# Inverse levels of the scan packed to 32 columns, with zero-padded 64x64 stationary blocks and the last level across row groups

## The chip, the cores and the metric

The kernel runs on one core of one Trainium2 chip. The metric is the device time of one execution in microseconds, the median of several runs. Engines are named as in the profile: PE (matrix products, PEld its weight loads), DVE (vector), ACT (scalar), POOL (GpSimd) and SP, which issues most DMAs. Each engine works through its own instructions in order; between engines there are only semaphores.

## What is computed

Two layers of a decoder trunk over 512 tokens of width 1024. Layer 0 mixes tokens with RWKV-7 (8 heads of 64) and gated DeltaNet (8 heads of 64), layer 1 with two kinds of attention, and each layer ends in a squared-ReLU MLP. The change touches only the chunked form of the two recurrences of layer 0. For a chunk of 64 tokens the reference of the DeltaNet half says:

```
a_mat = where(strict, einsum('bhnik,bhnjk->bhnij', k_beta, k) * decay, 0) + eye(C)
tri = partial(triangular_solve, left_side=True, lower=True, unit_diagonal=True)
u = tri(a_mat, v * beta);  w = tri(a_mat, k_beta * exp(g))
```

The kernel forms the inverse of the unit triangular 64x64 matrix instead of solving, for both recurrences: R stands for the RWKV half and G for the DeltaNet half. There are 8 heads x 2 chunks in a tile of 128 partitions x 512 columns (a chunk on each half of the partitions, a head on each 64 columns).

## The kernel before

Layer 0 first projects the inputs: 31 tiles of weights are loaded by SP, rounded by ACT (`tile_hi`, L1045), the rest of the split is computed by POOL (`tile_lo`, L1984), and PE multiplies. Between `tile_lo(3)` and `tile_lo(6)` POOL also builds constants: triangular masks in FULL, 128 partitions square for each of LEVELS = 6 levels, and from them MERGE, whose 64x64 blocks are copied for each half of the partitions (L2018 to L2021). SP loads tile u only after `tile_lo(u - 2)`.

Then comes the scan, `for s in range(TT + 1)` with TT = 4. Each engine has this loop with the calls written out by hand. In step s the products and the inverse of token block s are made ("ahead") while the state of block s - 1 is carried on and its output is made ("behind"). Step 0 has nothing behind, step 4 nothing ahead. The order on each engine is the order of the calls.

The inverse of a block doubles the size of the inverted diagonal blocks per level. The start is Q = I - (L within blocks of two): DVE multiplies L by the mask MERGE[0] (L1630 for G, L1641 for R) and POOL adds the identity (L2052), DVE transposes it into T (L1652). `LAST` is 5. For `lev` 0 to 4:

- PE, `below_blocks`: X = L x T, in PSUM bank 0 for R and bank 1 for G (through `both_halves`, L640: 8 heads x 2 halves of 64x64 times 64x64)
- ACT, `below_blocks` (L1189): copy of X with factor -1, one instruction of 128x512 for each of R and G
- PE, `joined_blocks`: Q x X, into the same bank
- DVE, `joined_blocks`: `copy_predicated` under MERGE[lev + 1] into T (L1659), for R then G; then, but for the last level, the transposes of R and G into Q (L1664). The last level writes straight into Q, which raises inv_done.

`both_halves` also makes key_values, MKV (L1175 on ACT evicts it), and chunk_out. `head_products` (L632) makes the four raw products, `by_state` (L655), `one_half` (L648) and `outer` (L744) serve the state. On ACT, L1171 evicts the lower rows of R, L1184 the state reads, L1199 and L1201 compute the norms of the output with a table load each, L1207 and L1211 scale and evict the turned output. On DVE, L1635, L1639 and L1640 mask the products, L1682 to L1685 update the state, L1698 to L1704 begin the chunk output, L1611 and L1612 scale the next rows. SP loads the first weights of the output projection only after inv_done of the last block.

Of the kernel before, what the change touches and what calls it, by code (L numbers as in the profile page):

```python
# [29 lines left out]
P = 128  # L30
# [67 lines left out]
def trunk_kernel(nc, a, out):  # L98
    ctx = ExitStack()
    with ctx:  # L100
# [54 lines left out]
        MERGE = grid(o_merge, LEVELS, HD)  # L155
        INCLC, STRICTC, EYEC = (flat(o_merge + (LEVELS + i) * HD, HD) for i in range(3))
# [88 lines left out]
        LTR, LTG, TIR, TIG, XMR, XMG, DT = (by_head(home("inverse")) for _ in range(7))  # L245
# [8 lines left out]
        MK = DT  # L254
        QC_KC, AD_RD = flat(o_gqkv, 8 * W), flat(o_kk, 8 * W)
# [59 lines left out]
        def p_reads(q):  # L315
# [44 lines left out]
        (inv_m, inv_q0, inv_x, inv_xm, inv_y, inv_t, inv_q, inv_done) = (sem(n) for n in (  # L360
            "inv_m inv_q0 inv_x inv_xm inv_y inv_t inv_q inv_done").split())
# [121 lines left out]
        def _(pe):  # L483
# [213 lines left out]

            def below_blocks(s, lev):

                n = 2 * LAST * s + 2 * lev  # L700
                for g, (lt, ti) in enumerate(((LTR, TIR), (LTG, TIG))):
                    pe.wait_ge(inv_t, n + (2 if lev == 0 else g + 1))
                    both_halves(g, lt, ti, True).then_inc(inv_x, 1)

            def joined_blocks(s, lev):
                n = 2 * LAST * s + 2 * lev
                for g, (qi, xm) in enumerate(((QIR, XMR), (QIG, XMG))):
                    pe.wait_ge(inv_xm, n + g + 1)
                    if lev == 0:
                        pe.wait_ge(inv_q0, 2 * s + 2)  # L710
                    else:
                        pe.wait_ge(inv_q, 2 * (LAST - 1) * s + 2 * (lev - 1) + g + 1)
                    if lev < LAST - 1:
                        both_halves(g, qi[s % 2], xm, True).then_inc(inv_y, 1)
                    else:
                        both_halves(g, xm, qi[s % 2], True).then_inc(inv_y, 1)
# [279 lines left out]
        def _(act):  # L996
# [221 lines left out]
            for s in range(TT + 1):  # L1218
# [195 lines left out]
        def _(dve):  # L1414
# [206 lines left out]
            def gated_products(s):  # L1621
# [8 lines left out]
                dve.tensor_tensor(QIG[s % 2], LTG, mask(MERGE[:, 0, :]), mul).then_inc(inv_m, 1)  # L1630
# [6 lines left out]
            def key_products(s):  # L1637
# [3 lines left out]
                dve.tensor_tensor(QIR[s % 2], LTR, mask(MERGE[:, 0, :]), mul).then_inc(inv_m, 1)  # L1641
# [481 lines left out]
```

## Time and profile before

| | |
|---|---|
| median of 3 runs | 1543.94 us (1543.9 to 1547.18) |
| profiled execution | 1542.63 us, its span 1540.7 us |
| mean granted clock of PE | 0.97 of full |
| busy: PE, PEld | 1440.3 us (93%), 1153.7 us |
| busy: DVE, ACT, POOL | 677.3, 605.4, 571.3 us |
| `L640 PE MATMUL 64*64 64x64 f32`, inputs in lower | x2112, 73.4 us busy, mean 228 ns |

A row of the timeline is the start, the time, the engine, the line, the operation with its shapes, and in square brackets how long the engine stood idle before it and who released it. "x2" merges instructions that follow one another; their time is then that of the run. An operation of fp32 on PE shows as two records, so that a group of `both_halves` has 32. The scan lies between about 220 and 442 us of the span. Steps 0 to 3 begin about 220, 255, 305 and 356 us.

### The profile page before, as it was taken

The page shows a single profiled execution, that of the slowest core. Times are in us where ns is not written, and L with a number is a line of the kernel's source. Part 1 is how long each engine was busy: PE and PEld are TensorE (multiplying, and loading weights), DVE is VectorE, ACT ScalarE, POOL GpSimd, SP SyncE. Part 2 cuts the span into 40 slices and gives each one's busy share as a digit, 9 for nine tenths or more (in the row PEclk, how much of TensorE's full clock was granted, in tenths as well). Part 3 has the DMA queues.
Part 4 walks back from the last instruction along what each step waited for, and adds up shares of the span by engine and source line. Part 5 has one row for each costly group of instructions (what it writes and reads, how often), then busy time and mean ns, then how long its engine had stood idle before and what let it go on. Part 6 is the DMA issues. An engine that isn't in the chain of part 4 may idle for free.

```text
span 1540.7 us, 24474 instructions
## 1 busy us (share of the span) xinstructions
PE 1440.3 (93%) x10273; PEld 1153.7 (75%) x10273; DVE 677.3 (44%) x1059; ACT 605.4 (39%) x872; POOL 571.3 (37%) x265
## 2 busy tenths in 40 slices
PE   7999899888769999999999799978999999999998
PEld 5787568788758888888888687754468888888886
DVE  4675756777543413223143306868823314122231
ACT  5425453434354413223142435467834313232231
POOL 4543321101024343434334232417934343434341
PEclk9999899999779999999999899998999999999999
DMA  4332200000112323232323221210012323223231
GB/s 141 96 96 68 69 14 3 3 3 3 57 55 84 108 84 107 83 100 91 107 84 83 82 83 56 82 55 1 1 55 83 109 82 104 88 93 97 85 106 54
DMA packets 128392, 109.99 MB, mean 71 GB/s; under 512 B 10679, under 2 KB 126513, under 8 KB 128305
## 3 DMA queue, kind: packets, MB, share of 16 engines
q1 hardware_dynamic: 127712, 107.64, 22.6%
q8 instruction: 69, 1.13, 0.3%
q10 hardware_dynamic: 592, 1.07, 0.2%
q14 instruction: 19, 0.15, 0.0%
HBM read 106.60 MB, written 2.10 MB: 71 GB/s over the span
## 4 chain that ended last, share of the span: by engine, by line
PE 76%; DVE 11%; ACT 5%; POOL 3%; issue 3%; DMA 1%; DVEq 0%; ACTq 0%; SPq 0%; POOLq 0%
PE ps L503 21%; PE ps L508 21%; PE ps L504 21%; PE ps L640 5%; POOL lower L2093 2%; DVE lower L1880 2%; DVE lower L1876 1%; PE ps L655 1%; PE ps L648 1%; POOL pw_lo L1984 1%; DVE lower L1865 1%; ACT lower L1377 1%; PE ps L744 1%; PE ps L617 1%; PE ps L540 1%
## 5 line engine op out<-in xcount | busy, mean ns | idle before, releaser
L2061 POOL TENSOR_TENSOR w_lo<-lower,w_hi 128x2048 fp32r<-128x2048 f32 x84 | 387.8, 4616 | 634.7 <-ACT w_hi L1033 634.7
L503 PE MATMUL ps<-h_hi,w_hi 128*128 128x512 f32 x792 | 316.3, 399 | 8.9 <-ACT h_hi L1038 5.9
L504 PE MATMUL ps<-h_hi,w_lo 128*128 128x512 f32 x792 | 315.0, 398 | 0.0
L1033 ACT ACTIVATE w_hi<-lower 128x2048 fp32r<-128x2048 f32 x84 | 160.2, 1907 | 242.8 <-PE ps L508 242.8
L508 PE MATMUL ps<-h_lo,w_hi 128*128 128x512 f32 x792 | 201.6, 396 | 0.3
L503 PE MATMUL ps<-a_hi,w_hi 128*128 128x512 f32 x480 | 189.3, 394 | 0.0
L504 PE MATMUL ps<-a_hi,w_lo 128*128 128x512 f32 x480 | 189.2, 394 | 0.0
L503 PEld LDWEIGHTS ps<-h_hi,w_hi 128*128 128x128 f32 x792 | 150.5, 190 | 46.4 <-issue 11.5
L504 PEld LDWEIGHTS ps<-h_hi,w_lo 128*128 128x128 f32 x792 | 150.6, 190 | 36.0 <-issue 0.5
L508 PEld LDWEIGHTS ps<-h_lo,w_hi 128*128 128x128 f32 x792 | 148.9, 188 | 37.2 <-DVE h_lo L1582 1.7
L1825 DVE TENSOR_TENSOR lower<-lower,ps 128x512 f32<-128x512 f32 x64 | 44.0, 688 | 268.7 <-PE ps L508 268.7
L1809 DVE SCALAR_TENSOR_TENSOR lower<-ps,lower 128x512 f32<-128x512 f32 x64 | 44.3, 692 | 226.0 <-PE ps L508 209.9
L1264 ACT ACTIVATE lower<-lower 128x512 f32<-128x512 f32 x64 | 40.5, 633 | 215.9 <-DVE lower L1809 215.9
L508 PE MATMUL ps<-a_lo,w_hi 128*128 128x512 f32 x480 | 121.5, 395 | 0.0
L1984 POOL TENSOR_TENSOR pw_lo<-lower,pw_hi 128x1024 fp32r<-128x1024 f32 (+1 forms) x31 | 76.2, 2460 | 118.4 <-ACT pw_hi L1045 118.2
L508 PEld LDWEIGHTS ps<-a_lo,w_hi 128*128 128x128 f32 x480 | 90.3, 188 | 21.6
L504 PEld LDWEIGHTS ps<-a_hi,w_lo 128*128 128x128 f32 x480 | 90.2, 188 | 21.2
L503 PEld LDWEIGHTS ps<-a_hi,w_hi 128*128 128x128 f32 x480 | 90.1, 188 | 21.1
L1814 DVE TENSOR_TENSOR h_lo<-lower,h_hi 128x512 fp32r<-128x512 f32 x64 | 97.4, 1521 | 6.9 <-ACT h_hi L1266 6.9
L503 PE MATMUL ps<-x_hi,pw_hi 128*128 128x512 f32 (+1 forms) x232 | 94.4, 407 | 0.4 <-POOL pw_lo L1984 0.4
L504 PE MATMUL ps<-x_hi,pw_lo 128*128 128x512 f32 (+1 forms) x232 | 91.5, 394 | 0.0
L640 PE MATMUL ps<-lower 64*64 64x64 f32 x2112 | 73.4, 228 | 11.6 <-DVE lower L1659 7.9
(356 smaller groups left out, 1974.0 us busy)
## 6 DMA issues: line engine op xcount, KB each, us to landing
lower<-in_mlp_w_dram SPq DMA_DIRECT2D x64, 1024.0 KB, 5.4
lower<-in_ev_w_in_dram SPq DMA_DIRECT2D x30, 512.0 KB, 3.9
lower<-in_od_w_in_dram SPq DMA_DIRECT2D x10, 1024.0 KB, 5.1
lower<-in_ev_w_out_dram SPq DMA_DIRECT2D x4, 1024.0 KB, 5.1
lower<-in_od_w_out_dram SPq DMA_DIRECT2D x4, 1024.0 KB, 4.9
out_dram<-lower SPq DMA_DIRECT2D x4, 512.0 KB, 3.2
lower<-in_od_w_in_dram SPq DMA_DIRECT2D x6, 256.0 KB, 3.8
upper<-in_x_dram SPq DMA_DIRECT2D x1, 1024.0 KB, 7.2
```

Of the source, the lines that this page charges most:

```text
L503: pe.matmul(o, wh, xh, start=(i_ == 0), stop=False)
L504: pe.matmul(o, wl, xh, start=False, stop=False)
L508: mm = pe.matmul(o, wh, xl, start=False, stop=(i_ == n_ - 1))
L640: mm = pe.matmul(ps[part, b, h_ * HD:(h_ + 1) * HD], mats[part, j, q, :], vals[part, j, q, :], start=(start and h_ == 0), stop=True, skip_ ...
L1033: act.activation(WH[:, u % 2, :, 0:w], RAW[:, u % 2, :, 0:w], ACT.Copy).then_inc(hi_ready, 1)
L1264: act.activation(sq, sq, ACT.Square).then_inc(h1_sq, 1)
L1809: dve.scalar_tensor_tensor(out=SQT[:, b % 4, :], in0=src(q)[:, :], scalar=0.0, in1=RS[2 * l + 1], op0=ALU.max, op1=mul).then_inc(bank_read, 1)
L1814: dve.tensor_tensor(HL[:, b, :], SQT[:, b % 4, :], as_f32(HH[:, b, :]), sub).then_inc(h1_ready, 1)
L1825: dve.tensor_tensor(XT[:, k, :], XT[:, k, :], src(q_m2[l] + k)[:, :], add)\
L1880: t.step(dve.match_replace(sc, M8[:, i, :], sc, TAKEN))
L1984: pool.tensor_tensor(PWL[:, u % 3, :, 0:w], PRAW[:, u % 2, :, 0:w], as_f32(PWH[:, u % 3, :, 0:w]), ALU.subtract).then_inc(pw_lo, 1)
L2061: pool.tensor_tensor(WL[:, u % 2, :, 0:w], RAW[:, u % 2, :, 0:w], as_f32(WH[:, u % 2, :, 0:w]), ALU.subtract)\
```

## The change

The diagonal 32x32 blocks are kept in compact form: Q (QCR, QCG) and its transpose (TCR, TCG) have 32 columns for each head, 128x256 in all, in place of 128x512. L is spread once into LDR and LDG, 64x64 per head, with zeros off the two diagonal 32x32 blocks; that is done on ACT by `sides`, two instructions with a factor of 0 or 1 for each partition (SIDE). In the inner levels (0 to 3) PE multiplies 64x64 stationary blocks with 32 moving columns (`in_halves`); ACT evicts X by `sides` with factors 0 and -1, again as a padded block, which becomes the stationary side of the second product. `copy_predicated` goes into the compact Q, and the transpose of that gives the moving side of the next level. In the last level PE works with 32x32 blocks that lie in different row groups (`across`), ACT copies compactly and then expands both Q into full width (four instructions, inv_exp), and DVE copies the lower left block in.

New ahead of the levels: ACT `diagonal` (a copy for each of G and R; the one for G stands before L1171 and waits for r_kk) and `spread` (four instructions, behind the eviction of MKV and before `solved(m, 1)`); DVE `diagonal` (a predicated copy and a multiplication for G behind L1635, for R behind L1640), where L1630 and L1641 go; POOL's addition becomes half as wide and also waits for inv_ld. POOL's constants lose the sixth level and the copies of MERGE, and gain JOIN, EYEQ and SIDE.

```diff
-        MERGE = grid(o_merge, LEVELS, HD)
-        INCLC, STRICTC, EYEC = (flat(o_merge + (LEVELS + i) * HD, HD) for i in range(3))
+        INCLC, STRICTC, EYEC = (flat(o_merge + i * HD, HD) for i in range(3))
+        HQ = HD // 2
+        JOIN = grid(o_merge + 3 * HD, LEVELS - 1, HQ)
+        EYEQ = flat(o_merge + 3 * HD + (LEVELS - 1) * HQ, HQ)
+        SIDE = flat(o_merge + 3 * HD + LEVELS * HQ, 4)
...
+            def in_halves(b, mats, vals):
+                for h_ in range(NH):
+                    j, q = h_ // 2, h_ % 2
+                    for part in HALVES:
+                        mm = pe.matmul(ps[part, b, h_ * HQ:(h_ + 1) * HQ], mats[part, j, q, :], vals[part, j, q, :],
+                                       start=True, stop=True)
+                return mm
+
+            def across(b, mats, vals, down):
+
+                for h_ in range(NH):
+                    j, q = h_ // 2, h_ % 2
+                    for k in range(2):
+                        first, second = (slice(k * HD + i * HQ, k * HD + (i + 1) * HQ) for i in range(2))
+                        rows, cols = (first, second) if down else (second, first)
+                        mm = pe.matmul(ps[cols, b, h_ * HQ:(h_ + 1) * HQ], mats[rows, j, q, :], vals[rows, j, q, :],
+                                       start=True, stop=True)
+                return mm
+
             def below_blocks(s, lev):
 
                 n = 2 * LAST * s + 2 * lev
-                for g, (lt, ti) in enumerate(((LTR, TIR), (LTG, TIG))):
+                for g, (lt, ld, tc) in enumerate(((LTR, LDR, TCR), (LTG, LDG, TCG))):
                     pe.wait_ge(inv_t, n + (2 if lev == 0 else g + 1))
-                    both_halves(g, lt, ti, True).then_inc(inv_x, 1)
+                    if lev < LAST - 1:
+                        pe.wait_ge(inv_ld, 2 * s + 2)
+                        in_halves(g, ld, tc).then_inc(inv_x, 1)
+                    else:
+                        across(g, lt[:, :, :, HQ:HD], tc, True).then_inc(inv_x, 1)
...
+            def sides(dst, src, neg, done):
+                act.activation(dst[:, :, :, 0:HQ], src, ACT.Copy, scale=SIDE[:, neg:neg + 1])
+                act.activation(dst[:, :, :, HQ:HD], src, ACT.Copy, scale=SIDE[:, neg + 1:neg + 2]).then_inc(done, 1)
+
+            def diagonal(s, g, lt, qc):
+                act.wait_ge(r_kk if g else r_lt, s + 1)
+                act.activation(qc, lt[:, :, :, 0:HQ], ACT.Copy).then_inc(inv_a, 1)
+
+            def spread(s):
+                for g, (ld, qc) in enumerate(((LDG, QCG), (LDR, QCR))):
+                    act.wait_ge(inv_c, 2 * s + g + 1)
+                    sides(ld, qc, 0, inv_ld)
+
             def below_blocks(s, lev):
-                for g, xm in enumerate((XMR, XMG)):
+                for g, (xe, ld) in enumerate(((QIR[s % 2], LDR), (QIG[s % 2], LDG))):
                     act.wait_ge(inv_x, 2 * LAST * s + 2 * lev + g + 1)
-                    act.activation(flat4(xm), bank[g], ACT.Copy, scale=-1.0).then_inc(inv_xm, 1)
+                    if lev < LAST - 1:
+                        sides(xe, quarter(g), 2, inv_xm)
+                    else:
+                        act.activation(compact(ld), quarter(g), ACT.Copy, scale=-1.0).then_inc(inv_xm, 1)
+                if lev == LAST - 1:
+                    for g, (qi, qc) in enumerate(((QIR[s % 2], QCR), (QIG[s % 2], QCG))):
+                        act.wait_ge(inv_q, 2 * (LAST - 1) * s + 2 * (LAST - 2) + g + 1)
+                        sides(qi, qc, 0, inv_exp)
...
                 if ahead:
+                    diagonal(s, 1, LTG, QCG)
                     lower_rows(s)
+                    diagonal(s, 0, LTR, QCR)
                     key_values(s)
+                    spread(s)
...
+            def diagonal(s, g, lt, qc, tc):
+                dve.wait_ge(inv_a, 2 * s + g + 1)
+                dve.copy_predicated(qc, on_side(1), lt[:, :, :, HQ:HD]).then_inc(inv_c, 1)
+                dve.wait_ge(inv_c, 2 * s + g + 1)
+                dve.tensor_tensor(tc, qc, of_quarter(JOIN[:, 0, :]), mul).then_inc(inv_m, 1)
...
             def joined_blocks(s, lev):
                 n = 2 * LAST * s + 2 * lev
                 inner = lev < LAST - 1
-                for g, x in enumerate((TIR, TIG) if inner else (QIR[s % 2], QIG[s % 2])):
+                for g, (qc, qi) in enumerate(((QCR, QIR[s % 2]), (QCG, QIG[s % 2]))):
                     dve.wait_ge(inv_y, n + g + 1)
-                    dve.copy_predicated(x, blocks(MERGE[:, lev + 1, :]), by_head(bank[g]))\
-                       .then_inc(inv_t if inner else inv_done, 1)
+                    if inner:
+                        dve.copy_predicated(qc, of_quarter(JOIN[:, lev + 1, :].bitcast(I32)), quarter(g))\
+                           .then_inc(inv_q, 1)
+                    else:
+                        dve.wait_ge(inv_exp, 2 * s + g + 1)
+                        dve.copy_predicated(qi[:, :, :, HQ:HD], on_side(0), quarter(g)).then_inc(inv_done, 1)
                 if inner:
-                    for g, (ti, qi) in enumerate(((TIR, QIR), (TIG, QIG))):
-                        dve.wait_ge(inv_t, n + 2 + g + 1)
-                        dve.transpose(flat4(qi[s % 2]), flat4(ti)).then_inc(inv_q, 1)
+                    for g, (tc, qc) in enumerate(((TCR, QCR), (TCG, QCG))):
+                        dve.wait_ge(inv_q, 2 * (LAST - 1) * s + 2 * lev + g + 1)
+                        dve.transpose(flat4(tc), flat4(qc)).then_inc(inv_t, 1)
...
             for part in HALVES:
-                t.link(pool.tensor_copy(MERGE[part], FULL[part, :, part]))
                 t.link(pool.tensor_copy(INCLC[part], INCL[part, part]))
                 t.link(pool.tensor_copy(EYEC[part], IDENT[part, part]))
             t.link(pool.tensor_tensor(STRICTC, INCLC, EYEC, ALU.subtract))
+            for i in range(4):
+                rows = slice(i * HQ, (i + 1) * HQ)
+                t.link(pool.tensor_copy(JOIN[rows], FULL[rows, 0:LEVELS - 1, rows]))
+                t.link(pool.tensor_copy(EYEQ[rows], IDENT[rows, rows]))
+                for at_, v_ in enumerate((1 - i % 2, i % 2, i % 2 - 1, -(i % 2))):
+                    t.link(pool.memset(SIDE[rows, at_:at_ + 1], float(v_)))
```

## Rows read from the trace of the kernel before

**Rows 1.** Chain that ended last, 200 to 470 us: start, time, what
```profile
230.95 1.28 POOL upper L2052
...
233.03 21.32 PE ps L640 x640
```

**Rows 2.** Timeline of ACT, 262 to 306 us (step 1): start, time, engine, line, operation
```profile
263.61 1.02 ACT L1184 ACTIVATE lower<-ps 64x1024 f32<-64x1024 f32 x1 [0.36 <-PE ps L655]
...
283.95 0.60 ACT L1189 ACTIVATE lower<-ps 128x512 f32<-128x512 f32 x1 [6.48 <-PE ps L640]
...
287.80 0.60 ACT L1189 ACTIVATE lower<-ps 128x512 f32<-128x512 f32 x1 [2.32 <-PE ps L640]
...
300.27 1.07 ACT L1189 ACTIVATE lower<-ps 128x512 f32<-128x512 f32 x2
301.22 1.51 ACT L1207 ACTIVATE lower<-ps,lower 128x128 f32<-128x128 f32 x4
302.59 0.72 ACT L1211 ACTIVATE upper<-ps,lower 128x512 f32<-128x512 f32 x1
```

**Rows 3.** Timeline of DVE, 285 to 308 us (step 1)
```profile
285.81 0.73 DVE L1659 COPY_PREDICATED lower<-lower,ps 128x512 f32<-128x512 int32 x1 [3.97 <-PE ps L640]
286.75 0.73 DVE L1659 COPY_PREDICATED lower<-lower,ps 128x512 f32<-128x512 int32 x1 [0.20 <-PE ps L640]
287.37 1.29 DVE L1664 STREAM_TRANSPOSE lower<-lower 128x512 f32<-128x512 f32 x2
288.59 0.65 DVE L1698 TENSOR_TENSOR lower<-lower 128x512 f32<-128x512 f32 x1
...
292.61 1.33 DVE L1659 COPY_PREDICATED lower<-lower,ps 128x512 f32<-128x512 int32 x2
```

**Rows 4.** Timeline of POOL, 38 to 50 us (constants)
```profile
39.22 0.55 POOL L1967 TENSOR_SCALAR_AFFINE_SELECT lower<-lower 128x64 f32<-128x64 f32 x2
...
42.19 0.60 POOL L2013 MEMSET lower<- 128x1 f32 x16
...
43.02 0.50 POOL L2018 COPY lower<-lower 64x384 f32<-64x384 f32 x1
...
43.88 0.23 POOL L2020 COPY lower<-lower 64x64 f32<-64x64 f32 x1
...
45.79 4.78 POOL L1984 TENSOR_TENSOR pw_lo<-lower,pw_hi 128x1024 fp32r<-128x1024 f32 x2
```

**Rows 5.** Chain that ended last, 38 to 62 us
```profile
50.60 5.11 DMA lower<-in_ev_w_in_dram
...
58.93 3.24 PE ps L579 x7
```

**Rows 6.** Timeline of PE, 106.6 to 107.45 us
```profile
106.82 0.39 PE L586 MATMUL ps<-lower 128*128 128x32 f32 x2
107.13 0.43 PE L589 MATMUL ps<-lower 128*64 128x32 f32 x8
```

**Rows 7.** Records of L589: duration min/median/max ns, first and last start us, form
```profile
L589 PE MATMUL ps<-lower x8: 222/223/243, 107.1 to 107.3; 128*64 128x32 f32 x8
```

**Rows 8.** Timeline of DVE, 262 to 275 us (step 1, ahead of the levels)
```profile
266.33 0.43 DVE L1683 TENSOR_TENSOR upper<-upper,lower 128x256 f32<-128x256 f32 x1
266.68 0.41 DVE L1685 TENSOR_TENSOR upper<-upper,ps 128x256 f32<-128x256 f32 x1
...
267.86 0.68 DVE L1640 TENSOR_TENSOR upper<-ps,lower 128x512 f32<-128x512 f32 x1
```

**Rows 9.** Timeline of PE, 226 to 240 us (step 0)
```profile
230.42 1.94 PE L640 MATMUL ps<-upper,lower 64*64 64x64 f32 x32 [1.50 <-DVE upper L1640]
...
233.03 3.68 PE L640 MATMUL ps<-lower 64*64 64x64 f32 x64 [0.66 <-DVE lower L1652]
...
238.81 1.39 PE L640 MATMUL ps<-lower 64*64 64x64 f32 x40
```

**Rows 10.** Stretches: time, busy of PE, PEld, DVE, ACT, POOL, granted clock, DMA, GB/s
```profile
230.00:235.00 5.00, 3.92 (x69) 3.76 (x70) 2.21 (x4) 0.60 (x1) 2.27 (x2) 0.55 0.01 3
...
340.00:345.00 5.00, 2.17 (x48) 2.03 (x46) 4.93 (x10) 1.26 (x2) 0.00 (x0) 0.81 0.02 3
```

More of the change, by code:

```diff
@@ L242, in of_tokens @@
             return x[:, :, s * P:(s + 1) * P].rearrange("p j (q t) -> p j q t", q=2)
-        LTR, LTG, TIR, TIG, XMR, XMG, DT = (by_head(home("inverse")) for _ in range(7))
+        LTR, LTG, LDR, LDG, DT = (by_head(home("inverse")) for _ in range(5))
+        QCR, QCG, TCR, TCG = (home("inverse", 2 * P).rearrange("p (j q t) -> p j q t", j=PAIRS, q=2) for _ in range(4))
         GTRI = by_head(home("even"))
@@ L254, in trunk_kernel, with compact, quarter @@
         MK = DT
+        def compact(x):
+            return x.rearrange("p j q t -> p (j q t)")[:, 0:2 * P].rearrange("p (j q t) -> p j q t", j=PAIRS, q=2)
+        def quarter(b):
+            return bank[b][:, 0:2 * P].rearrange("p (j q t) -> p j q t", j=PAIRS, q=2)
         QC_KC, AD_RD = flat(o_gqkv, 8 * W), flat(o_kk, 8 * W)
@@ L359, in trunk_kernel @@
              "e_sqg e_sqr e_var e_ln e_rstd e_on r_tr r_tg").split())
[L360 to L361 removed]
+        (inv_a, inv_c, inv_ld, inv_m, inv_q0, inv_x, inv_xm, inv_y, inv_t, inv_q, inv_exp, inv_done) = (
+            sem(n) for n in "inv_a inv_c inv_ld inv_m inv_q0 inv_x inv_xm inv_y inv_t inv_q inv_exp inv_done".split())
         LAST = LEVELS - 1
@@ L1998, in _ @@
             select(first, 0, [[-2, P // 2]], 1, 0.0, ALU.is_equal)
-            for lev in range(1, LEVELS):
+            for lev in range(1, LEVELS - 1):
                 if lev == 3:
@@ L2002, in _ @@
                 b = 1 << lev
-                last = int(lev == LEVELS - 1)
-                low = FULL[:, lev, :].rearrange("p (n q w) -> p n q w", q=2, w=b)[:, :, last, :]
-                t.link(pool.memset(low, 1.0))
-                select(low, 0 if last else -b, [[-2 * b, P // (2 * b)], [0, b]], 1, 0.0)
-                select(low, b - 1 if last else 2 * b - 1, [[2 * b, P // (2 * b)], [0, b]], -1, 0.0)
+                right = FULL[:, lev, :].rearrange("p (n q w) -> p n q w", q=2, w=b)[:, :, 1, :]
+                t.link(pool.memset(right, 1.0))
+                select(right, 0, [[-2 * b, P // (2 * b)], [0, b]], 1, 0.0)
+                select(right, b - 1, [[2 * b, P // (2 * b)], [0, b]], -1, 0.0)
             tile_lo(5)
@@ L2049, in _ @@
                     pool.memset(SG, 0.0).then_inc(e_state, 1)
-                for g, qi in enumerate((QIG, QIR)):
+                for g, (qc, tc) in enumerate(((QCG, TCG), (QCR, TCR))):
                     pool.wait_ge(inv_m, 2 * s + g + 1)
-                    pool.tensor_tensor(qi[s % 2], qi[s % 2], of_heads(EYEC), ALU.add).then_inc(inv_q0, 1)
+                    pool.wait_ge(inv_ld, 2 * s + g + 1)
+                    pool.tensor_tensor(qc, tc, EYEQ.unsqueeze(1).unsqueeze(1).broadcast_to([P, PAIRS, 2, HQ]),
+                                       ALU.add).then_inc(inv_q0, 1)
                 if s < TT - 1:
```

26 lines of the change are left out of this document (12 added, 14 removed).

## The prediction

> **What bounds the kernel now.** I read the chain of work that ended last, then each engine in order of time. The scan of layer 0 (about 220 to 442 us) is the only stage whose arithmetic changes. In the chain it is mostly L640, the helper behind all products of the inverse [rows 1]: in step 0 one piece of 21.32 us holds the whole inverse. So in step 0 every microsecond counts, while in steps 1 to 3 other work lies between the levels. One level repeats every 3.85 us (283.95 to 287.80 on ACT) [rows 2]; the four groups of products in it take 0.93 us each (two copies on DVE, each released by its group, start at 285.81 and 286.75) [rows 3], so 3.73 of 3.85 us are PE. A small gain of DVE or ACT is worth nothing there unless PE gets faster, and any stretch of latency is paid at once. A second place matters: POOL. The constants that it builds between two weight splits fill it from 42.19 to 45.79 us [rows 4], and the chain goes on from them through the next splits, a load of 5.11 us and ACT to PE's L579 [rows 5].
>
> **Constants, on the path.** POOL now builds four JOIN copies (32 partitions x 160), four EYEQ copies (x 32) and sixteen one-column memsets, each waiting for the one before. The 64x384 copy took 0.50 us and the 64x64 copy 0.23 [rows 4], so 0.31 and 0.20, with 0.06 us between links; a one-column memset is 0.10 (16 of them overlapped in 0.60, with 0.04 between starts) [rows 4], linked 0.16. Added: 4 x (0.37 + 0.26) + 16 x 0.16 = 5.1 us. Gone: two big copies (2 x 0.56) and the sixth mask, whose two selects took 0.55 [rows 4] and its memset with the links 0.3. Net 3.1 us in front of the split at 45.79. Behind it the chain goes from the second split straight to the load and on [rows 5], and PE's later tiles only queue behind L579. So I take all of it: **+3.1**. Bounds: 1.5, if one-column links cost half, to 4.
>
> **The products.** Each fp32 product shows as two records, 32 records a group. Inner levels keep a 64x64 stationary block and halve the moving columns to 32. The trace has that shape: L589, 64 columns stationary and 32 moving, 8 records in 0.43 us [rows 6]; one record is 0.22 [rows 7], so the three steps between its four pairs are 0.07 each, the first, which starts the stream, the longest. L586 has 128 stationary and 32 moving columns: two records in 0.39, some 0.11 to 0.16 apart by the same reckoning [rows 6]. The pitch follows the stationary width, not the moving one, and today's group with 64 moving columns is 16 pairs in 0.93, 0.058 each. So I take 0.93 for an inner group after the change, too: **no gain on PE**. The other bound is 0.47, if in this tiling the moving side sets it. In the last level the blocks are 32 wide: 0.47 by width, 0.93 by count. I take 0.6.
> For that last level a rule speaks against a gain: the Trainium skill, "TensorEngine Tiling (Array Packing)", Instruction Overhead, says that a matmul of one column takes as long as one of 60 and that a dimension already small should not be tiled. As an estimate from that page, 60 cycles for each of 32 records is 0.8 us at full clock instead of my 0.6; the sum would be 0.8 us higher (two groups on the path in steps 0 and 3). No row here has this shape.
>
> **The inner cycle.** Dependencies change: `copy_predicated` now fills the compact QC, and the moving operand TC is its transpose. DVE's order is copy R, copy G, transpose R, transpose G, so the next level waits for both copies and a transpose; before, it waited for copy R alone. DVE: a 128x256 operation is 0.41 to 0.43 with 0.35 between starts, 0.27 less than the 0.68 of a 128x512 [rows 8]; the 512-wide copy and transpose are 0.73 and 0.68 [rows 3], so 0.46 and 0.42. ACT: one eviction of 0.60 becomes two with a per-partition scale. Such a 128x512 is 0.72; 512 columns more cost 0.43 (1.02 against 0.59 to 0.60), so 256 less give 0.50; four 128x128 take 1.51, 0.35 apart [rows 2], so with 128 columns more 0.40 between starts and 0.9 us for both. From the start of a level: group R lands at 1.15, ACT to 2.08, joined R 2.13 to 3.28; joined G starts at 3.07 and lands at 4.17; copy G at 4.22, transpose R 4.58 to 5.00, next level at 5.04. That is **+1.19 per level** where nothing covers it.
>
> **Step 0, uncovered.** (a) ACT's new copy waits for r_kk, and behind it in its queue stands L1171, the lower rows, for which L1635 waits: +0.45. DVE then does copy and multiply for G (0.85, 0.1 of it slack) before L1639: key values on PE start at 231.6 instead of 230.42 [rows 9]. They land at 233.5 (cold clock), ACT copies MKV (0.6, 0.48 to the next start), then spreads L (4 x 0.40 + 0.1): 235.8; POOL adds the identity in 0.75 (1.27 for double width [rows 1]); transpose: the first level starts at 237.1 instead of 233.03 [rows 9]: **+4.05**. (b) Level 0 ran mostly at a clock near half (0.55 [rows 10]; 64 records in 3.68 us [rows 9]) and took 5.78 us. The new cycle is 8.1 cold (groups of 1.75) and 5.04 warm; if the clock rises about 4 us after PE restarts, as it did, 6.9: **+1.1**. (c) Levels 1 to 3: 3 x 1.19 = **+3.6**. (d) Last level: smaller evictions, copies and products: **-0.5** (0 to -0.9). Sum 8.2.
>
> **Steps 1 to 3.** (a) Front: the new copy on ACT pushes L1171 back by 0.3; on DVE copy and multiply (0.85) stand before the state sums, so L1640 ends at 269.35, not 268.54 [rows 8]; PE's key values wait for that: +0.81. The mask multiply L1630 that falls away was hidden behind ACT. Queued behind are the chunk's state reads, which move with it. The spread on ACT (to 273.0) and POOL's add lie in PE's work until 275.6 and cost nothing; if that cover went, 1 us. (b) Level 0: ACT +0.29. (c) Level 1 is 1.19 longer on PE, but level 2 is bound by DVE's chunk output: from L1698 (288.59) to the copy at 292.61, 4.02 us [rows 3]. L1698 can start 5.26 us after level 1 instead of 5.77, since copies and transposes are narrower; then 4.02 and 1.19 to the next level: 10.48 instead of 10.57, so -0.09, and both extra waits of PE are hidden. (d) After level 3 ACT's two table loads and exponentials bound the step (up to 300.27 [rows 2]), and that eviction is 0.28 later: +0.28. (e) At the end DVE's two copies go from 1.33 [rows 3] to 0.82, unless the last products or the four new expansions on ACT (4 x 0.40) come later, which today are not there: -0.1 to -0.5, taken -0.35. That is **+0.94** each for steps 1 and 2. In step 3 PE was last at the end, so the cheaper last level gives -0.7: **+0.6**.
>
> **Sum**: 3.1 + 8.2 + 1.9 + 0.6 = 13.8 us. The profiled execution took 1542.63 us (span 1540.7): 1556.4. The three runs have median 1543.94, 1.3 above it; I forecast **1556.5**.
>
> **Rivals.**
> 1. *The moving side sets the pace*: inner groups 0.47. For: 64 and 32 are both half of something here and L589 is only 8 records. Against: L586 and L589 [rows 6, 7]. The cycle is then 4.10 (step 0: 3 x 0.25; ACT and DVE bound it), step 0 costs 4.5, steps 1 to 3 give back 1.1 each because L1698 starts 1.4 earlier: 3.1 + 4.5 - 3.3 = +4.3, **1547**.
> 2. *The clock falls*: PE now stands about 1 us in every level. The granted clock fell in step 2 after a stand of 2.8 us (0.81 in 340 to 345 [rows 10]), but not in step 1 after the same stand. At the low level a cycle is 8.1, 3.0 more. One more cold level a step is +12: **1568**; all of them near +30. It decides where the gaps together make PE count as idle. The reverse is in it, too: the stand before level 3 shrinks from 2.8 to about 1.4 us, and the two falls of steps 2 and 3, 1.4 us each, could go: 1553.6, inside my forecast.
> 3. *Faster*: rival 1, with POOL's constants covered by a load that lands sooner, and the two clock falls of steps 2 and 3 gone: 4.3 - 3.1 - 2.9 = -1.7 against the profile's 1542.6, and with step 0's spread overlapped by PE's cold products 2 less, **1539**. Against it: the chain through POOL [rows 5]. It wins once groups are at 0.5 or less.
> 4. *The change doesn't do what it says*: the narrower DVE work is all on covered stretches and so are the additions; within 2 us, **1545**.
>
> **How the numbers follow.** Forecast with its clock variant 60% (1551 to 1561 for itself), rival 1 12%, rival 2 15%, rival 3 7%, rival 4 6%. The range leaves out the deep end of rival 2, rival 3 and half of rival 4: 1545.5 to 1568. Against 1543.94, 0.2% (3.1 us, what a measurement can tell) puts faster at 7%; within at 11% (rival 4 and the low half of rival 1), slower at 82%.
>
> **What would show it.** Groups of L640's successor: evictions of R and G 0.93 apart in inner levels (step 1, level 1) if the stationary side binds, under 0.6 if not. In step 0 a level every 5.0 us. PE's first level of step 0 some 4 us later after its key values than now, after the fourth spread on ACT. The split behind POOL's constants near 48.9 instead of 45.79, and L579 as much later. Level 3 of step 1 no later relative to level 1. What would make it wrong: groups at half length, a clock near 0.5 through the levels, or POOL's one-column links far from 0.16 us.

## The result and the profile after

The changed kernel takes **1599.28 us** (median of 4 runs, 1595.2 to 1602.73) against 1543.92 for the kernel before, measured beside it: 1.0355 times as long, with a 95% interval of 1.0329 to 1.0382. I had forecast 1556.5, at most 1568. The direction was right, the size was not: 43 us are missing from the sum. The profiled execution took 1602.73 us with a span of 1601.0 and a mean granted clock of 0.924 (0.97 before); it is the slowest of the four, so sums over its steps come to 60 us of loss where the medians give 55.

In what follows a stand is a stretch of time in which PE has nothing to do and waits for another engine, and a fall is a stretch in which its granted clock goes from 1.00 to 0.50.

The first thing to look at is the clock. Stretches of step 0, the kernel before and then the kernel after (columns as in [rows 10]):

```profile
240.00:250.00 10.00, 10.00 (x342) 9.92 (x338) 7.17 (x12) 4.31 (x8) 0.16 (x1) 1.00 0.02 5
```
```profile
240.00:250.00 10.00, 9.12 (x172) 8.99 (x172) 1.54 (x4) 2.48 (x6) 0.00 (x0) 0.50 0.01 2
250.00:260.00 10.00, 9.12 (x173) 8.99 (x170) 2.13 (x5) 2.55 (x7) 0.00 (x0) 0.50 0.01 3
260.00:270.00 10.00, 9.12 (x170) 8.96 (x168) 1.99 (x5) 2.84 (x6) 1.82 (x2) 0.50 0.01 2
```

PE is busy for 9.12 of 10 us, but it issues half as many records, at a granted clock of 0.50, which is its level of 1.2 GHz. Before, the clock was back at 1.00 from 237.3 us on and stayed there until 343.1, in step 2. The timeline of PE in the kernel after shows the levels that follow from it; they answer to [rows 9]:

```profile
239.31 3.62 PE L713 MATMUL ps<-lower 64*64 64x32 f32 x64 [3.62 <-DVE lower L1712]
...
247.23 3.63 PE L713 MATMUL ps<-lower 64*64 64x32 f32 x64 [0.88 <-DVE lower L1728]
...
255.15 3.63 PE L713 MATMUL ps<-lower 64*64 64x32 f32 x64 [0.88 <-DVE lower L1728]
...
270.99 3.46 PE L724 MATMUL ps<-lower 32*32 32x32 f32 x128 [0.88 <-DVE lower L1728]
275.61 2.05 PE L677 MATMUL ps<-upper,lower 128*128 128x512 f32 x2 [1.16 <-DVE upper L1724]
```

A level repeats every 7.92 us. It is the cold cycle of my sum (8.1) in all four inner levels, where I had the clock rise within the first. From the second level on each has a stand of 0.88 us in front of it, which DVE's transpose ends.

Two other views answer to [rows 2] and [rows 4]. ACT in step 1, a level at full clock, and POOL at the constants:

```profile
313.59 0.47 ACT L1217 ACTIVATE lower<-ps,lower 128x256 f32<-128x256 f32 x1 [10.22 <-PE ps L713]
313.96 0.47 ACT L1218 ACTIVATE lower<-ps,lower 128x256 f32<-128x256 f32 x1
314.53 0.47 ACT L1217 ACTIVATE lower<-ps,lower 128x256 f32<-128x256 f32 x1
```
```profile
44.89 0.31 POOL L2088 COPY lower<-lower 32x160 f32<-32x160 f32 x1
45.26 0.20 POOL L2089 COPY lower<-lower 32x32 f32<-32x32 f32 x1
45.52 0.53 POOL L2091 MEMSET lower<- 32x1 f32 x4
...
49.82 0.12 POOL L2092 MEMSET lower<- 128x16 f32 x1
50.01 4.71 POOL L2050 TENSOR_TENSOR pw_lo<-lower,pw_hi 128x1024 fp32r<-128x1024 f32 x2
```

The groups of R and G are 0.94 us apart (313.59 to 314.53): 32 moving columns gain nothing at full clock.

The table gives, for each profiled run, the start of the scan (PE's first product of step 0, L666 or its like), the length of each step from one such product to the next, steps 3 and 4 together up to DVE's first operation on the finished rows, the rest of the span, and how long the clock was at 0.50 between 215 and 530 us by the clock record. The kernels are those of the experiments below. The medians are over all executions, the other columns are of the one that was profiled.

| kernel | median us | scan starts | step 0 | 1 | 2 | 3 and 4 | rest | at 0.50 |
|---|---|---|---|---|---|---|---|---|
| before | 1543.9 | 220.0 | 35.2 | 49.9 | 51.4 | 86.7 | 1097.5 | 44 |
| after | 1599.3 | 223.0 | 52.6 | 63.4 | 65.2 | 99.2 | 1097.7 | 195 |
| e1 | 1569.1 | 222.9 | 42.0 | 55.0 | 54.8 | 94.6 | 1097.5 | 92 |
| e2 | 1570.3 | 220.5 | 47.2 | 54.5 | 54.5 | 94.2 | 1097.7 | 116 |
| e3 | 1562.8 | 223.8 | 40.3 | 54.4 | 54.6 | 91.1 | 1097.6 | 85 |
| e4 | 1548.7 | 225.8 | 34.8 | 49.9 | 51.3 | 86.7 | 1097.4 | 41 |
| e5 | 1568.1 | 223.1 | 43.7 | 54.2 | 54.6 | 93.3 | 1096.0 | 75 |
| e6 | 1558.1 | 224.1 | 40.6 | 55.0 | 54.5 | 85.6 | 1095.8 | 31 |
| e7 | 1537.6 | 221.8 | 33.3 | 51.4 | 51.4 | 82.8 | 1095.3 | 10 |
| e8 | 1541.4 | 223.2 | 37.8 | 51.4 | 51.1 | 80.8 | 1095.2 | 7 |
| e9 | 1532.3 | 221.4 | 33.3 | 49.9 | 49.9 | 81.4 | 1095.9 | 0 |
| e10 | 1551.6 | 220.9 | 35.4 | 50.2 | 54.6 | 90.1 | 1097.4 | 58 |
| e11 | 1546.3 | 223.6 | 37.8 | 53.3 | 52.3 | 83.8 | 1094.5 | 27 |
| e12 | 1546.6 | 224.0 | 40.5 | 51.4 | 50.6 | 81.7 | 1096.7 | 3 |
| e13 | 1567.3 | 223.1 | 49.9 | 55.8 | 57.4 | 84.6 | 1094.6 | 72 |
| e14 | 1591.7 | 223.7 | 49.7 | 58.3 | 58.3 | 99.2 | 1096.8 | 150 |

Nearly all of the loss lies in the scan: 3.0 us ahead of it, 17.4, 13.5, 13.8 and 12.5 in the steps, 0.2 behind. And the time at 0.50 grew by 150 us. The start of the scan alone lies between 220.0 and 221.8 us in the five kernels whose work ahead of it is that of before, so the 3.0 is good to about 1 us.

### The profile page after: what moved, and what is told of

Read it like the earlier page. It is cut to its first block, busy times and chain, and to the rows that moved or that the text cites. A ratio compares the mean times of both kernels' runs of the same rounds, so it can differ in the third digit from the quotient of the medians.

```text
span 1601.0 us, 24581 instructions
## 1 busy us (share of the span) xinstructions
PE 1491.4 (93%) x10273; PEld 1201.3 (75%) x10273; DVE 659.5 (41%) x1067; ACT 627.0 (39%) x944; POOL 570.0 (36%) x284
## 4 chain that ended last, share of the span: by engine, by line
PE 77%; DVE 10%; ACT 6%; POOL 3%; issue 2%; DMA 1%; DVEq 0%; ACTq 0%; SPq 0%; POOLq 0%
PE ps L519 20%; PE ps L514 20%; PE ps L515 20%; PE ps L713 6%; POOL lower L2165 2%; DVE lower L1946 1%; PE ps L666 1%; DVE lower L1942 1%; PE ps L651 1%; PE ps L628 1%; PE ps L659 1%; ACT lower L1430 1%; PE ps L724 1%; POOL pw_lo L2050 1%; DVE lower L1931 1%
## 5 line engine op out<-in xcount | busy, mean ns | idle before, releaser
L1317 ACT ACTIVATE lower<-lower 128x512 f32<-128x512 f32 x64 | 40.5, 633 | 215.9 <-DVE lower L1875 215.9
L515 PEld LDWEIGHTS ps<-a_hi,w_lo 128*128 128x128 f32 x480 | 90.1, 188 | 21.4
L515 PE MATMUL ps<-x_hi,pw_lo 128*128 128x512 f32 (+1 forms) x232 | 91.1, 393 | 0.0
L713 PE MATMUL ps<-lower 64*64 64x32 f32 x1536 | 74.9, 268 | 11.6 <-DVE lower L1728 7.9
```

Of the source, the lines that this page charges most:

```text
L515: pe.matmul(o, wl, xh, start=False, stop=False)
L713: mm = pe.matmul(ps[part, b, h_ * HQ:(h_ + 1) * HQ], mats[part, j, q, :], vals[part, j, q, :], start=True, stop=True)
L1317: act.activation(sq, sq, ACT.Square).then_inc(h1_sq, 1)
```

## The experiments

**e1: the columns sent twice.** In the changed kernel:

```diff
-                        mm = pe.matmul(ps[part, b, h_ * HQ:(h_ + 1) * HQ], mats[part, j, q, :], vals[part, j, q, :],
+                        mm = pe.matmul(ps[part, b, h_ * HD:(h_ + 1) * HD].rearrange("p (a t) -> p a t", a=2),
+                                       mats[part, j, q, :],
+                                       vals[part, j, q, :].unsqueeze(1).broadcast_to([HD, 2, HQ]),
```

> The changed kernel, with each inner product of the inverse sent its 32 moving columns twice (64 columns into the full bank, of which ACT and DVE read the first 32 of each 64). The work that is used, the waits and the order are those of the changed kernel. Theory 1, the granted clock stays at 0.50 because only 32 columns move behind each 64-wide stationary block: the clock is back at 1.00 from the second level of step 0 on, as before the change, an inner level of step 0 takes 5.0 to 5.1 us, and the time is my forecast's sum, 1553 to 1560 us. Theory 2, the stands of 0.9 us that the longer chain of DVE and ACT leaves in every level make the clock fall: the stands are still there, so the clock stays at 0.50 and the time within 5 us of 1599. Theory 3, the padded blocks themselves cost the time: also near 1599.

Measured: 1569.11 us, 1.0152 (1.0124 to 1.0181). More work for PE, and 30 us less time. Stretches of step 0, and its levels on PE:

```profile
240.00:250.00 10.00, 9.11 (x248) 8.69 (x244) 2.00 (x5) 3.35 (x8) 0.00 (x0) 0.85 0.01 3
250.00:260.00 10.00, 8.23 (x258) 7.76 (x256) 3.68 (x9) 4.37 (x10) 0.45 (x1) 1.00 0.01 3
```
```profile
245.89 2.08 PE L716 MATMUL ps<-lower 64*64 64x64 f32 x64 [0.88 <-DVE lower L1733]
...
250.94 2.08 PE L716 MATMUL ps<-lower 64*64 64x64 f32 x64 [0.88 <-DVE lower L1733]
...
261.03 2.38 PE L729 MATMUL ps<-lower 32*32 32x32 f32 x128 [0.88 <-DVE lower L1733]
```

The clock is back at 1.00 and a level takes 5.05 us, with the same stands of 0.88. Theory 1 holds for step 0 but not in its time, and theories 2 and 3 fall. 13 us above my sum remain: the clock still falls, most of all near the step ends (263 to 270, 315 to 325, 369 to 380) and for 48 us from 424 us on.

**e2: only the columns halved, in the kernel before.** Half of each inner product is left out. `in_halves` is here the loop of `both_halves` with `vals[part, j, q, 0:HD // 2]` as its moving side, and the inner levels of `joined_blocks` go through it, too:

```diff
-                    both_halves(g, lt, ti, True).then_inc(inv_x, 1)
+                    (in_halves(g, lt, ti) if lev < LAST - 1 else both_halves(g, lt, ti, True)).then_inc(inv_x, 1)
```

> The kernel before, with the inner products (levels 0 to 2 and 3 of 5, all but the last) sent only the first 32 of their 64 moving columns; half of each inner product is left out, and the output is not the reference's. No wait, no order and no operation of another engine changes, and PE still stands for nothing between the groups of a level. Theory 1: a group at full clock keeps its 0.93 us (no gain from fewer columns), but in step 0 the clock doesn't rise to 1.00 after its first level as it does before the change, and much of the four inverses runs at 0.50: slower than before, 1565 to 1590 us. Theory 2 (stands decide): the clock is that of before, and the time 1544 within 3 us. Theory 4, the moving side sets the pace of a group: groups near 0.5 us and the time below 1541.

Measured: 1570.26 us, 1.0165 (1.0143 to 1.0186). Half of the columns taken away, no wait added, 26 us lost. Stretches and timeline of PE in e2:

```profile
240.00:250.00 10.00, 10.00 (x194) 10.00 (x191) 5.13 (x8) 1.79 (x3) 0.00 (x0) 0.50 0.01 2
250.00:260.00 10.00, 10.00 (x192) 10.00 (x192) 3.25 (x5) 2.95 (x5) 1.12 (x1) 0.50 0.02 3
```
```profile
257.44 3.60 PE L702 MATMUL ps<-lower,upper 64*64 64x32 f32 x64
260.86 3.66 PE L640 MATMUL ps<-lower 64*64 64x64 f32 x64
264.31 2.53 PE L640 MATMUL ps<-upper,lower 64*64 64x64 f32 x64
```

From 235 to 260 us PE is busy without a pause and the clock stays at 0.50. It rises at 265.4 us, inside the last level, which still has 64 columns. So once PE is at the low clock, these products with 32 columns did not bring it back here.

**e3: DVE's order, on top of e1.** In `joined_blocks` on DVE:

```diff
                            .then_inc(inv_q, 1)
+                        dve.wait_ge(inv_q, 2 * (LAST - 1) * s + 2 * lev + g + 1)
+                        dve.transpose(flat4((TCR, TCG)[g]), flat4(qc)).then_inc(inv_t, 1)
...
-                if inner:
-                    for g, (tc, qc) in enumerate(((TCR, QCR), (TCG, QCG))):
-                        dve.wait_ge(inv_q, 2 * (LAST - 1) * s + 2 * lev + g + 1)
-                        dve.transpose(flat4(tc), flat4(qc)).then_inc(inv_t, 1)
```

> The same as the kernel with its columns sent twice, and DVE's order in the inner levels is copy R, transpose R, copy G, transpose G, so that the next level waits for one copy and one transpose. The stand of PE between two levels goes from about 0.9 to 0.2 us. Theory 1: an inner level of step 0 takes about 4.4 us instead of 5.05, three of them count, and the time is 1 to 3 us under that kernel's, with the clock alike. Theory 2: the clock is low where the stands are 0.9 and full here, so this one is some 40 us faster than the other.

Measured: 1562.75 us, 1.0103 (1.0075 to 1.0131), 6.4 us under e1. An inner level takes 4.26 us. The gain is more than the 1 to 3 us of theory 1 and far from the 40 of theory 2: 1.7 in step 0 and 3.5 in steps 3 and 4, where less time is at 0.50.

**e4: POOL's constants alone, in the kernel before.** Behind its `tensor_tensor(STRICTC, ...)`:

```diff
+            for i in range(4):
+                rows = slice(i * HQ, (i + 1) * HQ)
+                t.link(pool.tensor_copy(JOIN[rows], FULL[rows, 0:LEVELS - 1, rows]))
+                t.link(pool.tensor_copy(EYEQ[rows], IDENT[rows, rows]))
+                for at_, v_ in enumerate((1 - i % 2, i % 2, i % 2 - 1, -(i % 2))):
+                    t.link(pool.memset(EYEQ[rows, at_:at_ + 1], float(v_)))
```

> The kernel before, and on POOL, in the place where the change builds them, the added constants alone: four copies of 32 x 160, four of 32 x 32 and sixteen linked one-column memsets, 5.1 us by my prices, with nothing removed. My forecast's step: all of it lies on the path, since the chain goes through POOL's next split, so the time is +4.5 to +5.5 us, 1548.5 to 1549.5. The rival: the loads of weights cover it, and the time is that of before within 1 us.

Measured: 1548.66 us, 1.0031 (1.0021 to 1.0041), +4.5 us; the added operations took 4.95 us on POOL and the steps of the scan are those of before. The step of my forecast holds: nothing covers them.

**e5: the last level twice, on top of e3.** In `across`:

```diff
-                        mm = pe.matmul(ps[cols, b, h_ * HQ:(h_ + 1) * HQ], mats[rows, j, q, :], vals[rows, j, q, :],
+                        for again in range(2):
+                            mm = pe.matmul(ps[cols, b, h_ * HQ:(h_ + 1) * HQ], mats[rows, j, q, :],
```

> The kernel with its columns sent twice and DVE in the order copy R, transpose R, copy G, transpose G (1562.75 us), and in addition each small product of the last level is issued twice, into the same place. A group of the last level goes from about 0.53 to 1.06 us at full clock, near the 0.93 that it took before the change; nothing else changes. In the kernel without this the clock fell to 0.50 for 10 us around the last level of steps 0 to 2 (279 to 290, 314 to 324, 368 to 378 in its trace) and for 20 and 17 us at the end. Theory 1, the small last level takes away work that kept the clock up: these falls go, except those that the kernel before had, too; steps 1 and 2 take 51 to 52 us instead of 54.5, and the time is 1552 to 1557, although PE does 2 us more in each step. Theory 2, the falls come from the stands at the end of a step and not from the small products: the clock falls as it did and the time is 1562 to 1567.

Measured: 1568.06 us, 1.0165 (1.0147 to 1.0183). Theory 1 fails: the falls at 279, 314 and 368 us went, others came (265 to 271, 336 to 347, 374 to 381), and 5 us were lost. Theory 2 comes within 1.1 us with its time (1562 to 1567), but its reason doesn't hold, as the falls did not stay where they were.

**e6: filler on top of e5.** The same function serves all later kernels:

```diff
+            def filler(b, n):
+                for i in range(n):
+                    pe.matmul(bank[b][:, 0:P], HEADS2, IDENT, start=True, stop=True)
```

It is called ahead of a wait, as `filler(7, 6)` in front of `pe.wait_ge(r_lt, s + 1)`, with a bank whose readers are done.

> The kernel of the run with the last level twice, and in addition products that nobody reads (128 columns, HEADS2 by IDENT, into a bank that is free) in the stands of PE: 5, 2, 10 and 16 ahead of the first level of step 0, 6 ahead of level 3 in steps 1 to 3, a few at the step ends, 10, 5 and 3 in the last chunk, 44 and 12 behind it. By 0.21 us each they fit into the stands. It shows what the change costs once the clock is held. Theory 1: the mean granted clock of the scan is near 1.00, what is left over the kernel before is the longer front of step 0, the longer cycle and POOL's constants, and step 0 takes 38 to 40 us: 1543 to 1550. Theory 2, the clock isn't moved by such work or the filler delays what it stands before: 1555 or more.

Measured: 1558.07 us, 1.0097 (1.0081 to 1.0114). That is theory 2's time, but not its first reason: the filler does move the clock, 31 us at 0.50 instead of the 75 of e5, and 10 us are won. Steps 3 and 4 are short (85.6), but steps 1 and 2 still take 55.0 and 54.5: PE's stands ahead of the key values are open, with 7, 10 and 10 us at 0.50 from about 15 us into each of steps 1 to 3, and the last level is doubled.

**e7: filler in the kernel before.**

> The kernel before with the same kind of filler in PE's stands: 5, 2, 6 and 6 ahead of the first level of step 0, 12 (2.6 us in a stand of 2.8) ahead of level 3 in steps 1 to 3, 3 and 2 at the step ends, 10, 5 and 3 in the last chunk, 44 behind it and 12 before the output projection. The kernel before spends 44 us of the scan at 0.50: 230 to 237, 343 to 347, 394 to 398, 411 to 425 and 432 to 449. Theory 1, work of any use keeps the clock: these go, at 3.4, 1.7, 1.7, about 5 and 3 us, and the time is 1528 to 1536. Theory 2, the clock is cut by power or time and not by what PE does: the falls stay or move elsewhere, and the time is 1542 to 1548.

Measured: 1537.56 us, 0.9961 (0.9947 to 0.9975). The clock follows the filler: 10 us at 0.50 instead of 44. The time misses my range by 1.6, since a new fall of 3.4 us came in each of steps 1 to 3, behind the stands that I had left open.

**e8: the change with every stand filled** (e3 and filler; 9 products ahead of the key values of steps 1 to 3 and 3 ahead of the second chunk's solved values).

> The change with its columns sent twice, DVE in the order copy R, transpose R, copy G, transpose G, the last level's products issued once, and the filler of the run before, to which 9 products ahead of the key values of steps 1 to 3 (a stand of 2.3 us there) and 3 ahead of each second chunk's solved values (0.9 us) are added. In every version of the change so far level 0 of steps 1 to 3 started 22.9 to 25.9 us after its step, against 19.56 before the change, with a fall of the clock in each. Theory 1, my forecast's front (+0.81) is right by itself and the fall of the clock is what it triggers, since PE's stand ahead of the key values grows by it: with the stand filled the clock holds, level 0 starts at 20.4 to 20.8, steps 1 and 2 take 50.5 to 51.5 us, and the time is 1545 to 1551. Theory 2, the front is longer by another wait: level 0 starts after 22.5 even at full clock, and the time is 1553 or more.

Measured: 1541.44 us, 0.9984 (0.9975 to 0.9993), 21 us under e3 and less than expected. Theory 1 holds: 7 us at 0.50 in the whole scan, and the first level of steps 1 to 3 starts 20.35, 21.45 and 20.34 us after the step's first product (19.56 before the change; the fall of 7 us lies in step 1's end and step 2's start).

**e9: the kernel before with every stand filled.**

> The kernel before with the filler of the earlier run (1537.56 us, clock low for only 3.4 us in each of steps 1 to 3, in the dense work behind the key values) and in addition 6 products ahead of the key values of steps 1 to 3 (a stand of 1.5 us) and 3 ahead of each second chunk's solved values (0.9 us). Theory 1: these stands were what the clock fell for; the three falls go, steps 1 and 2 take 49.9 instead of 51.4 us, and the time is 1532 to 1535. Theory 2: the filler delays more than the clock gives back, or the falls move: 1536 to 1540.

Measured: **1532.32 us, 0.9927** (0.9913 to 0.994), the fastest of all; the products that were added are read by nobody. Stretches where [rows 10] showed 0.55 and 0.81, and one behind the scan, first of e9, then the last one of the kernel before:

```profile
230.00:235.00 5.00, 5.00 (x88) 4.51 (x82) 3.54 (x6) 0.60 (x1) 3.35 (x3) 1.00 0.01 3
...
340.00:345.00 5.00, 5.00 (x100) 4.85 (x102) 4.93 (x10) 1.94 (x4) 0.00 (x0) 1.00 0.01 3
...
440.00:450.00 10.00, 10.00 (x45) 8.09 (x44) 4.77 (x6) 4.08 (x6) 4.62 (x1) 1.00 0.29 91
```
```profile
440.00:450.00 10.00, 7.05 (x20) 5.30 (x19) 6.89 (x11) 7.71 (x14) 1.30 (x1) 0.55 0.01 2
```

The filler, 6 products (12 records) in 1.60 us, fits into the stands (timeline of PE in e9); the key values begin 10.4 us after the step, as before:

```profile
230.21 1.60 PE L664 MATMUL ps<-lower 128*128 128x128 f32 x12
231.78 1.15 PE L640 MATMUL ps<-upper,lower 64*64 64x64 f32 x32
232.86 1.60 PE L664 MATMUL ps<-lower 128*128 128x128 f32 x12
234.40 2.08 PE L640 MATMUL ps<-lower 64*64 64x64 f32 x64
```

**e10: two more DVE operations ahead of the key products, in the kernel before.**

```diff
                 dve.tensor_tensor(RBM[s], product_of(2, 1), mask(INCLC), mul).then_inc(r_rbm, 1)
+                if s > 0:
+                    for x in (XMR, XMG):
+                        dve.tensor_tensor(x[:, :, :, 0:HD // 2], LTG[:, :, :, 0:HD // 2], LTG[:, :, :, HD // 2:HD], mul)
```

> The kernel before with two more DVE operations of 256 columns (0.43 us each, read by nobody) in steps 1 to 3, where the change has its predicated copy and its multiply: between the bonus rows and the key products. PE's key values come 0.8 us later and its stand ahead of them is 2.3 instead of 1.5 us; all products are those of before. My forecast's step: the delay is all there is, level 0 of steps 1 to 3 starts 0.8 us later (20.4 instead of 19.56) and the time is +2 to +3 us, 1546 to 1547. The rival, found in the traces of the change: the longer stand makes the clock fall for the dense work behind it, level 0 starts after 22.9 to 23.3 us in each of the three steps, and the time is +8 to +12, 1552 to 1556.

Measured: 1551.62 us, 1.0057 (1.0039 to 1.0076). The key values came only 0.34 us later, and step 1 is 0.3 longer. In steps 2 and 3 the same delay went with two falls each, the first from 320.4 us on:

```profile
320.00:325.00 5.00, 3.71 (x66) 3.64 (x67) 1.78 (x4) 0.60 (x1) 2.27 (x2) 0.66 0.01 3
325.00:330.00 5.00, 4.87 (x92) 4.74 (x93) 2.80 (x5) 2.20 (x3) 0.00 (x0) 0.73 0.02 3
```

Step 2 is 3.2 us longer than before. The time lies between the two expectations, 0.4 us under the rival's. The rival's mechanism is seen in two steps of three, in the profiled execution; the four executions spread from 1549.2 to 1556.1.

**e11 and e12: e8 with 32 columns, and e8 with the change's own order.**

> The change with DVE's order copy R, transpose R, copy G, transpose G and the filler in PE's stands, but with its own 32 moving columns (in the run at 1541.44 us they were sent twice, and nothing else differs). The clock is full at the first level of step 0 here. Theory 1, the products with 32 columns do not keep the clock, also where PE never stands: it falls within the four inner levels of step 0 and again in the levels of steps 1 to 3, an inner level then takes 7.0 to 7.9 us, and the time is 1558 to 1590. Theory 2, the stands were the cause and the filler is enough: inner levels of 4.3 us and 1540 to 1544.

> The change with its columns sent twice and the filler, but with DVE's own order of the change (copy R, copy G, transpose R, transpose G); against the run at 1541.44 us only the order is undone, and PE stands 0.9 us in each inner level again. Against the kernel before with all its stands filled (1532.32 us) this is the change at a clock that is held on both sides, so it measures the sum of my forecast, 13.8 us. The clock holds: +0.8 for each of three levels in step 0 and a little in the others, 1543 to 1548. If stands of 0.9 us in each level make the clock fall even with 64 columns: 1552 or more.

Measured: e11 1546.26 us, 1.0008 (0.9995 to 1.0021); e12 1546.56 us, 1.0014 (1.0004 to 1.0024). In e11 theory 1 falls: inner levels of 4.2 us with 32 columns at full clock. Theory 2 misses its time by 2.3 us: what is left at 0.50 there are 6.8 us at each of the four last levels. Three of its ten executions took 1540.7 to 1541.9 us, with a higher mean clock (0.981, against 0.978 or less), so not all of these falls seem to come every time. In e12 the levels take 5.05 us at full clock. PE's levels of step 0, e11 and then e12:

```profile
244.21 2.06 PE L724 MATMUL ps<-lower 64*64 64x32 f32 x64
...
248.41 2.06 PE L724 MATMUL ps<-lower 64*64 64x32 f32 x64
```
```profile
245.44 2.08 PE L727 MATMUL ps<-lower 64*64 64x64 f32 x64 [0.88 <-DVE lower L1754]
...
250.48 2.08 PE L727 MATMUL ps<-lower 64*64 64x64 f32 x64 [0.88 <-DVE lower L1754]
```

**e13 and e14: the change as it is, with filler in its other stands, and with filler only ahead of step 0's first level.**

> The changed kernel as it is (32 moving columns, its own order, PE stands 0.9 us in each inner level) with nothing but the filler in the other stands. The runs so far held the clock in the inner levels with 64 columns and these stands (1546.56), with 32 columns and no stands (1546.26), and with 64 and none (1541.44); this is the fourth case. Theory 1, it takes both, few columns and a stand in every level: the clock, full at the first level of step 0, falls within the four levels, an inner level goes from 5.05 to 7.92 us, and the time is 1560 to 1585. Theory 2, only a level that starts cold stays cold with 32 columns: with a full start the clock holds in all inner levels, 5.05 each, and the time is 1546 to 1552.

> The changed kernel with filler only ahead of the first level of step 0 (5, 2, 10 and 16 products), so that the four inner levels of step 0 start at full clock; everything behind is the change as it is. Theory 1, it takes both, few columns and a stand in every level: the clock falls within step 0's levels all the same, and step 0 takes 46 to 52 us (52.6 in the change) and the time is 1590 to 1599. Theory 2, the cold start is what makes step 0 cold: an inner level is 5.05, step 0 takes 39 to 40 us, and the time is 1584 to 1590, with steps 1 to 3 as in the change (63, 65 us) since they come from their own stands.

Measured: e13 1567.31 us, 1.0146 (1.012 to 1.0172); e14 1591.65 us, 1.032 (1.0278 to 1.0361). Theory 1 holds in both. The timeline of PE in e13:

```profile
239.46 2.05 PE L724 MATMUL ps<-lower 64*64 64x32 f32 x64
241.52 2.06 PE L724 MATMUL ps<-lower,upper 64*64 64x32 f32 x64
244.45 3.60 PE L724 MATMUL ps<-lower 64*64 64x32 f32 x64 [0.88 <-DVE lower L1749]
247.86 3.61 PE L724 MATMUL ps<-lower,upper 64*64 64x32 f32 x64
252.34 3.63 PE L724 MATMUL ps<-lower 64*64 64x32 f32 x64 [0.87 <-DVE lower L1749]
```

The first level runs at full clock; at the first stand of 0.88 us the clock falls (244.5) and comes back only at 275.2.

Four kernels with all other stands filled, then, and what the pair gives: 64 columns without the stand 1541.4, 64 with it 1546.6, 32 without it 1546.3, 32 with it 1567.3. Each alone costs 5 us, both together 26. The two 5 us are not alike. With the stand alone (e12) the clock is at 0.50 for 3 us only, and 2.7 of the 5 us are the longer cycle itself, in step 0; 1.5 lie behind the scan, where the two kernels don't differ in what was changed. With the 32 columns alone (e11) the cycle is short and the clock is at 0.50 for 27 us. With both it is at 0.50 for 72.

## Why the prediction was wrong

**What was right.** The kernel's own steps came as priced:

- No gain on PE: groups 0.94 apart (forecast 0.93).
- The warm inner cycle 5.05 in e1 and e12 (5.04), the cold one 7.92 (8.1). ACT's two evictions start 0.37 apart and take 0.47 (0.40 and 0.50).
- POOL: 44.89 to 49.82 us, 4.93 for the 5.1 of additions. The split stands at 50.01 instead of 45.79, but 1.1 of that is there ahead of the constants, so 3.1 net, and the scan starts 3.0 us later.
- Front of step 0: the key values 11.55 us after the step instead of 10.40, +1.15 (+1.18), and the first level 16.3 instead of 13.0, +3.3 for +4.05. Last level of step 0 in e12 1.0 shorter than in e9 (-0.5).
- DVE's copy and multiply: key values of step 1 at 14.24 in e3, 13.45 before, +0.79 (+0.81).
- Last level: groups 0.53 us apart at full clock in e1 (four within 2.38 us), forecast 0.6. The 0.8 that I had estimated from the Trainium skill's "TensorEngine Tiling (Array Packing)", Instruction Overhead, doesn't hold here; the measurement decides.

**The sum was right where the clock is held.** e12 is the change with its columns sent twice and its other stands filled, e9 the kernel before with its stands filled. (No run has 32 columns, these stands and a clock that holds; that the columns make no difference to a group at full clock is shown by the 0.94 us above.) Their spans differ by 1544.9 - 1531.8 = 13.1 us, their medians by 14.2; my sum was 13.8. By steps: +2.6 ahead of the scan (3.1), +7.2 in step 0 (8.2), +1.5 and +0.7 in steps 1 and 2 (0.94 each), +0.3 in steps 3 and 4 (0.6), the other 0.8 behind the scan, where I had nothing. Half of the 1.5 in step 1 is not mine either: e12's one fall, 262.6 to 266.0 us, reaches into it and makes its key values 0.74 us later than in steps 2 and 3.

**The step that failed** is the clock, in two places. In "Step 0 (b)" I wrote "if the clock rises about 4 us after PE restarts, as it did": it rose behind products with 64 columns, and the change halves those columns. e2 shows that this alone keeps the four inner levels of step 0 at 0.50, with PE busy throughout. And rival 2, to which I gave 15%, was what happened, by a condition that I had only half: I named the stands of 1 us, not the columns, though I had worked out that their time doesn't shrink with them. e11 to e13 show that the stand and the 32 columns cost 5 us each where they come alone and 26 together. Its price was too small as well: "all of them near +30", and it is 43. That counted the inner levels alone. The clock was also low ahead of them: in the first 5.0, 3.0 and 6.2 us of steps 1 to 3, left over from the step before, and in step 2 again from 16.7 us on, just behind its key values. So the first level of these steps starts 23.2 to 25.1 us after the step instead of 19.6, of which +0.8 was the wait. And step 4 ran at 0.50 nearly throughout. e10 shows that a fall behind the key values can go with a delay of 0.34 us.

In time: from e12 to the change are 52.7 us. Filling its other stands wins 32.0 of them (1599.3 to 1567.3 in e13), and 64 columns in place of 32 the other 20.7 (e13 to e12).

In e2 PE was busy for 10.00 of 10.00 us and was granted 0.50. The Trainium skill, "TensorE: Matmul & The Clock Gate", Part 1, says that the gate goes by how busy PE has been; if that is read as the busy time of a profile, this run disagrees.

**What stays open.** Why e5 lost time, why e11 kept more of its clock in three executions of ten, and why in e10 step 1 kept the clock with the delay that cost steps 2 and 3 theirs: the falls may move with the phase of the work, but no run here sorts that out. e8 and e9 differ by 9.1 us (7.6 in the spans of their profiled executions), where my terms without the longer cycle of step 0's four inner levels give 13.8 - 4 x 0.8 = 10.6; no run splits the rest.

## What to carry to other kernels

Before PE gets less to do, or a wait more, read the granted clock around it and ask what holds it: here a saving on the moving side that did not shorten a product went with half of PE's speed, and a stand of 0.88 us together with it cost more than its length. Where a latency-bound stretch shows the low clock, put products that nobody reads into the stands, each a little shorter than its stand; here that alone gave 0.7%. And price a change at a held clock and at the low one as two cases of the whole, not as one level more or less.

## What the runs showed that I had not expected

- PE busy for 25 us without a pause at half clock (e2, 235 to 260 us), and full clock 4.5 us after the products went from 32 to 64 moving columns (260.86 to 265.4).
- Two causes that cost 5 us each and together 26 (e8, e11, e12, e13).
- More work made the kernel faster twice: 30 us by sending each column twice, 11.4 us by filler in the kernel before (1543.8 to 1532.3).
- Key values that came 0.34 us later on PE went with a loss of 7.9 us (e10).
